# Splitting the first attention's output projection along its contraction, with part of it multiplied between the attention units

## The reference, cut to what matters

```python
def block_fn(args):
    ...
    p = jax.nn.softmax(jnp.concatenate([s_band, s_ctx, s_sink_lat], axis=-1), axis=-1)
    ...
    o = jnp.einsum('bhgqk,bkhd->bqhgd', p_band, vb) + jnp.einsum('bhgqk,bkhd->bqhgd', p_ctx, vc)
    return o

o_blocks = lax.map(block_fn, (jnp.arange(nb), q_blocks))
o_lat = jnp.moveaxis(o_blocks, 0, 1).reshape(bsz, seq, N_HEADS * HEAD_DIM) @ w_o
...
h_lat = h_lat + g1 * y_lat
b_lat = modulate(rmsnorm(h_lat, norm2_g[i]), sh2, sc2)
```

## Time and profile before

| | |
|---|---|
| median of 3 runs | 2436.53 us |
| lowest, highest run | 2434.88, 2446.08 us |
| profiled execution, first to last instruction (its span) | 2433.2 us |
| that execution's own time | not given apart from its span |
| PE (TensorE matmul) busy in the span | 2276.1 us, 94% |
| PEld (weight load), DVE, ACT, POOL busy | 77%, 48%, 41%, 35% |
| first attention, first score to first `wo` matmul | 1042.7 to 1182.5 us |
| stage `wo` | 1182.5 to about 1225 us |

### The profile page before, as it was taken

How to read it: one execution, slowest core, us unless ns; L and a number is a source line. 1 busy time by engine, 2 the same in 40 slices (tenths; PEclk the granted TensorE clock), 3 DMA queues, 4 the chain that set the end, 5 groups by cost and what they waited for, 6 DMA issues and landing times.

```text
span 2433.2 us, 37255 instructions
## 1 busy us (share of the span) xinstructions
PE 2276.1 (94%) x14435; PEld 1872.0 (77%) x14435; DVE 1161.3 (48%) x2028; ACT 987.4 (41%) x1673; POOL 852.0 (35%) x445
## 2 busy tenths in 40 slices
PE   4999699999999998999989999989988889999998
PEld 4887487888888886767778888877746777778777
DVE  4699723432043335378444223447475536441441
ACT  5665544332133324378454324444353214332341
POOL 1799224222222234300144444433301114443443
PEclk9999798999999998999999999999898989999999
DMA  8888021222122221200123333332200002333332
GB/s 272 257 270 255 20 61 52 61 64 72 56 61 60 74 66 58 69 10 1 43 86 97 101 90 95 106 99 79 83 1 2 2 1 86 88 101 90 88 106 83
DMA packets 337090, 204.59 MB, mean 84 GB/s; under 512 B 5869, under 2 KB 335159, under 8 KB 336951
## 3 DMA queue, kind: packets, MB, share of 16 engines
q1 hardware_dynamic: 331915, 194.02, 26.7%
q10 hardware_dynamic: 5036, 8.66, 1.1%
HBM read 200.47 MB, written 2.19 MB: 83 GB/s over the span
## 4 chain that ended last, share of the span: by engine, by line
PE 60%; issue 20%; POOL 9%; DVE 5%; ACT 3%; DVEq 1%; SPq 1%; DMA 1%; ACTq 1%; POOLq 0%
PE ps L623 17%; PE ps L624 17%; PE ps L625 17%; POOL w_lo L550 6%; POOL pc L1610 2%; DVE ps L1578 1%; PE ps L1981 1%; PE ps L896 1%; DVE m L3209 1%; PE ps L2009 1%; PE ps L3008 1%; ACT w_hi L593 1%; DMA ada_x<-in_ada_w 1%; PE ps L1670 1%; SPq L774 0%
## 5 line engine op out<-in xcount | busy, mean ns | idle before, releaser
L550 POOL TENSOR_TENSOR w_lo<-raw,w_hi 128x1024 fp32r<-128x1024 f32 (+1 forms) x203 | 525.8, 2591 | 1105.4 <-ACT w_hi L593 1089.4
L623 PE MATMUL ps<-x_hi,w_hi 128*128 128x512 f32 (+1 forms) x1896 | 689.7, 364 | 30.3 <-DVE x_lo L1481 12.5
L624 PE MATMUL ps<-x_lo,w_hi 128*128 128x512 f32 (+1 forms) x1896 | 676.1, 357 | 0.0
L625 PE MATMUL ps<-x_hi,w_lo 128*128 128x512 f32 (+1 forms) x1896 | 674.6, 356 | 0.0
L593 ACT ACTIVATE w_hi<-raw 128x1024 fp32r<-128x1024 f32 (+1 forms) x251 | 280.3, 1117 | 520.3 <-PE ps L625 515.1
L623 PEld LDWEIGHTS ps<-x_hi,w_hi 128*128 128x128 f32 x1896 | 364.7, 192 | 98.1 <-issue 22.7
L624 PEld LDWEIGHTS ps<-x_lo,w_hi 128*128 128x128 f32 x1896 | 365.4, 193 | 52.3 <-issue 3.8
L625 PEld LDWEIGHTS ps<-x_hi,w_lo 128*128 128x128 f32 x1896 | 364.6, 192 | 50.2
L1855 DVE SCALAR_TENSOR_TENSOR f_a<-ps,prm,f_a 128x511 f32<-128x511 f32 (+2 forms) x176 | 116.1, 680 | 371.4 <-ACT f_b L1820 360.5
L623 PE MATMUL ps<-g_hi,w_hi 128*128 128x512 f32 (+1 forms) x704 | 257.1, 365 | 2.1 <-POOL w_lo L550 1.4
L624 PE MATMUL ps<-g_lo,w_hi 128*128 128x512 f32 (+1 forms) x704 | 255.8, 363 | 0.0
(11 more groups left out here) (388 smaller groups left out, 2966.0 us busy)
## 6 DMA issues: line engine op xcount, KB each, us to landing
raw<-in_ffn_w_up SPq DMA_DIRECT2D x88, 512.0 KB, 3.8
ada_tail<-in_ada_w SPq DMA_DIRECT2D x22, 1024.0 KB, 7.4
raw<-in_ffn_w_down SPq DMA_DIRECT2D x32, 704.0 KB, 4.6
raw<-in_w_up SPq DMA_DIRECT2D x44, 512.0 KB, 3.8
ada_s<-in_ada_w SPq DMA_DIRECT2D x20, 1024.0 KB, 7.9
raw<-in_conv_w_pw SPq DMA_DIRECT2D x24, 512.0 KB, 6.2
raw<-in_w_down SPq DMA_DIRECT2D x16, 704.0 KB, 4.6
raw<-in_w_in SPq DMA_DIRECT2D x17, 512.0 KB, 4.0
```

The costliest lines, as they stand in the source:

```text
L550: pool.tensor_tensor(M.w_lo[:, slot, 0:K * P], M.raw[:, slot, 0:K * P], M.w_hi[:, slot, 0:K * P].bitcast(F32), ALU.subtract).then_inc(lo_r ...
L623: pe.matmul(o, wh, hi[:, k, t0:t0 + tn], start=first, stop=False)
L624: pe.matmul(o, wh, lo[:, k, t0:t0 + tn], start=False, stop=False)
L625: return pe.matmul(o, wl, hi[:, k, t0:t0 + tn], start=False, stop=last)
```

## The change

The projection is now two streams. `woa` has 8 parts: K tiles 0 to 3 of output tiles 0 to 5, and K tiles 4 and 5 of output tiles 0 and 1. `wo` keeps the rest: K tiles 6 and 7 for output tiles 0 and 1, K tiles 4 to 7 for tiles 2 to 5, all eight for tiles 6 and 7 (`PARTS_OF`). The parts of `woa` are multiplied from unit step 40 on, one part in three steps: a third of its matmuls after the products of the first step, a third after the scores of each of the next two. The result gathers in PSUM bank 6, so the transposed pieces of this attention turn over two banks instead of three (`turn_banks=2`). Four steps after a part began, DVE adds it to `h`, and ACT rounds the weights of the part two ahead; POOL's subtraction and SP's load follow by the semaphores as before. Loads, roundings and subtractions are as wide as the part.

```diff
-STREAMS += [("qkv", 12, 8), ("wo", 8, 8)]
+STREAMS += [("qkv", 12, 8), ("woa", 8, 4), ("wo", 8, 8)]
...
+PARTS_OF = {"woa": [(m, 0, 4) for m in range(6)] + [(0, 4, 6), (1, 4, 6)],
+            "wo": [(m, (6, 6, 4, 4, 4, 4, 0, 0)[m], 8) for m in range(8)]}
...
-            sp.dma_start(M.raw[:, slot, 0:K * P].rearrange("p (k c) -> p k c", c=P),
-                         w_src[name][:, :, bass.ds(c, P)]).then_inc(s_raw[slot], 16)
+            k0, k1 = part_of(name, 4 * it + u)[1:] if name in PARTS_OF else (0, K)
+            sp.dma_start(M.raw[:, slot, 0:(k1 - k0) * P].rearrange("p (k c) -> p k c", c=P),
+                         w_src[name][:, k0:k1, bass.ds(c, P)]).then_inc(s_raw[slot], 16)
...
         def turn_ps(self, j):
-            return (TURN_BANK + j % 3) * 512
+            return (TURN_BANK + j % self.turn_banks) * 512
...
         for u in range(n_u + VALUES + 3):
             if u + 2 < n_u:
                 scores(u + 2)
+            if between:
+                between(u, 0)
             if 0 <= u - TURN < n_u:
                 turn(u - TURN)
             for quarter in range(4):
                 for g in X.groups_at(u, VALUES + quarter):
                     values(g, quarter)
+            if between:
+                between(u, 1)
...
-    ATT1 = Attention(groups1(), M.p1, M.pt1, (0, 0, 0, 0, 0))
+    ATT1 = Attention(groups1(), M.p1, M.pt1, (0, 0, 0, 0, 0), turn_banks=2)
+    WOA_BANK, WOA_AT, WOA_UNITS = 6, 40, 3
+    WOA = PARTS_OF["woa"]
...
+        def third(i, n):
+            _, k0, k1 = WOA[i]
+            todo = [(k, x) for k in range(k0, k1) for x in range(3)]
+            if n == 0:
+                pe.wait_ge(lo_ready, done(q0 + i + 1))
+                pe.wait_ge(evac, done(q0 + i))
+                pe.wait_ge(att_x, done(2 * k1))
+            for k, x in todo[n * len(todo) // 3:(n + 1) * len(todo) // 3]:
+                at = slice((k - k0) * P, (k - k0 + 1) * P)
+                w = (M.w_hi, M.w_hi, M.w_lo)[x][:, (q0 + i) % 2, at]
+                mm = pe.matmul(woa_ps(), w, (M.x_hi, M.x_lo, M.x_hi)[x][:, k, 0:SEQ], start=(k, x) == todo[0],
+                               stop=(k, x) == todo[-1])
+            if n == 2:
+                mm.then_inc(tile_done, 1)
+
+        def between(u, late):
+            i, n = (u - WOA_AT) // WOA_UNITS, (u - WOA_AT) % WOA_UNITS
+            if 0 <= i < len(WOA) and late == (n == 0):
+                third(i, n)
...
+        def between(u):
+            i, n = (u - WOA_AT - 4) // WOA_UNITS, (u - WOA_AT - 4) % WOA_UNITS
+            if n or not 0 <= i < len(WOA):
+                return
+            m = WOA[i][0]
+            dve.wait_ge(tile_done, done(q0 + i + 1))
+            o = M.h[:, m, 0:SEQ]
+            dve.scalar_tensor_tensor(out=o, in0=woa_ps(), scalar=M.mods[:, 48 + 16 + m, 0:1], in1=o, op0=ALU.mult,
+                                     op1=ALU.add).then_inc(evac, 1)
...
+            if n == 0 and 0 <= i < len(WOA):
+                high(act, "woa", i // 4, i % 4)
```

More of the change, by code:

```diff
@@ L80, with part_of @@
 N_CHUNKS = dict((s[0], s[1]) for s in STREAMS)
+PARTS_OF = {"woa": [(m, 0, 4) for m in range(6)] + [(0, 4, 6), (1, 4, 6)],
+            "wo": [(m, (6, 6, 4, 4, 4, 4, 0, 0)[m], 8) for m in range(8)]}
+for _name, _parts in PARTS_OF.items():
+    for _i, (_m, _k0, _k1) in enumerate(_parts):
+        ROWS_AT[Q0[_name] + _i] = _k1 - _k0
+def part_of(name, i):
+    return PARTS_OF[name][i] if name in PARTS_OF else (i, 0, ROWS_OF[name])
 Q_ALL = _q
@@ L480, in build_in @@
         order = order[:order.index(stop) + 1]
-    streams_of = {"pw1": ["pw1"], "pw2": ["pw2"], "qkv": ["qkv"], "wo": ["wo"],
+    streams_of = {"pw1": ["pw1"], "pw2": ["pw2"], "qkv": ["qkv"], "attn": ["woa"], "wo": ["wo"],
                   "w_in": ["mem_kv", "w_in"], "w_out": ["w_out"]}
@@ L492, in build_in @@
     w_src = {"pw1": rows(A["conv_w_pw1"][0], 8), "pw2": rows(A["conv_w_pw2"][0], 8),
-             "qkv": rows(A["attn_w_qkv"][0], 8), "wo": rows(A["attn_w_o"][0], 8),
+             "qkv": rows(A["attn_w_qkv"][0], 8), "wo": rows(A["attn_w_o"][0], 8), "woa": rows(A["attn_w_o"][0], 8),
              "w_in": rows(A["w_in_2"][0], 8), "mem_kv": rows(A["w_mem_kv_2"][0], 8),
@@ L508, in column @@
             return W_IN_ORDER[4 * it + u] * P
+        if name in PARTS_OF:
+            return part_of(name, 4 * it + u)[0] * P
         if name.startswith("up"):
@@ L523, in one @@
             sp.wait_ge(lo_ready, done(q0 + 4 * it + u - 1))
-            sp.dma_start(M.raw[:, slot, 0:K * P].rearrange("p (k c) -> p k c", c=P),
-                         w_src[name][:, :, bass.ds(c, P)]).then_inc(s_raw[slot], 16)
-        if full >= 2 and name not in ("qkv", "w_in"):
+            k0, k1 = part_of(name, 4 * it + u)[1:] if name in PARTS_OF else (0, K)
+            sp.dma_start(M.raw[:, slot, 0:(k1 - k0) * P].rearrange("p (k c) -> p k c", c=P),
+                         w_src[name][:, k0:k1, bass.ds(c, P)]).then_inc(s_raw[slot], 16)
+        if full >= 2 and name not in ("qkv", "w_in") and name not in PARTS_OF:
             with sp.Fori(0, full) as it:
@@ L547, in one @@
             slot = (q0 + u) % 2
+            w = ROWS_AT[q0 + 4 * it + u] * P if name in PARTS_OF else K * P
             pool.wait_ge(hi_ready, done(q0 + 4 * it + u + 1))
-            pool.tensor_tensor(M.w_lo[:, slot, 0:K * P], M.raw[:, slot, 0:K * P],
-                               M.w_hi[:, slot, 0:K * P].bitcast(F32), ALU.subtract).then_inc(lo_ready, 1)
+            pool.tensor_tensor(M.w_lo[:, slot, 0:w], M.raw[:, slot, 0:w],
+                               M.w_hi[:, slot, 0:w].bitcast(F32), ALU.subtract).then_inc(lo_ready, 1)
         if last is not None:
@@ L555, in low_stream @@
             return
-        if full >= 2:
+        if full >= 2 and name not in PARTS_OF:
             with pool.Fori(0, full) as it:
@@ L611, in moved, with tile_products @@
         return (M.xg_hi, M.xg_lo) if name.startswith("up2") else (M.x_hi, M.x_lo)
-    def tile_products(pe, name, u, t0, tn, k, at=None, ends=None):
+    def tile_products(pe, name, u, t0, tn, k, at=None, ends=None, k0=0):
         K, q0 = ROWS_OF[name], Q0[name]
@@ L617, in tile_products @@
         hi, lo = moved(name)
-        wh = M.w_hi[:, slot, k * P:(k + 1) * P]
-        wl = M.w_lo[:, slot, k * P:(k + 1) * P]
+        wh = M.w_hi[:, slot, (k - k0) * P:(k - k0 + 1) * P]
+        wl = M.w_lo[:, slot, (k - k0) * P:(k - k0 + 1) * P]
         at = t0 if at is None else at
@@ L637, in products @@
         for n, (t0, tn) in enumerate(segs):
+            if name in PARTS_OF:
+                _, k0, k1 = part_of(name, 4 * it + u)
+                for k in range(k0, k1):
+                    mm = tile_products(pe, name, u, t0, tn, k, ends=(k == k0, k == k1 - 1), k0=k0)
+                continue
             for k in range(ROWS_OF[name]):
@@ L1942, in build_in, with __init__ @@
     class Attention:
-        def __init__(self, groups, p, pt, before):
+        def __init__(self, groups, p, pt, before, turn_banks=3):
             self.groups, self.p, self.pt = groups, p, pt
+            self.turn_banks = turn_banks
             self.units = [x for g in groups for x in g.heads]
@@ L1970, in turn_ps, with att_pe @@
         def turn_ps(self, j):
-            return (TURN_BANK + j % 3) * 512
-    def att_pe(pe, X):
+            return (TURN_BANK + j % self.turn_banks) * 512
+    def att_pe(pe, X, between=None):
         n_u = len(X.units)
@@ L1988, in turn @@
                 j = X.piece[u] + m
-                if j >= 3:
-                    eng, count = X.pieces[j - 3]
+                if j >= X.turn_banks:
+                    eng, count = X.pieces[j - X.turn_banks]
                     if eng == "A":
@@ L2036, in bring_out, with att_dve @@
                  M.ps[:, at:at + nk].rearrange("p (t k) -> p t k", k=P)).then_inc(brought, 1)
-    def att_dve(dve, X):
+    def att_dve(dve, X, between=None):
         n_u = len(X.units)
@@ L2070, in att_dve @@
                 negated(u)
+            if between:
+                between(u)
             if 0 <= u - 1 < n_u:
@@ L2076, in att_dve, with att_act @@
                 low(g)
-    def att_act(act, X):
+    def att_act(act, X, between=None):
         n_u = len(X.units)
@@ L2283, in groups1, with woa_ps, woa_pe, woa_dve @@
         return out_
-    ATT1 = Attention(groups1(), M.p1, M.pt1, (0, 0, 0, 0, 0))
+    ATT1 = Attention(groups1(), M.p1, M.pt1, (0, 0, 0, 0, 0), turn_banks=2)
+    WOA_BANK, WOA_AT, WOA_UNITS = 6, 40, 3
+    WOA = PARTS_OF["woa"]
+    def woa_ps():
+        return M.ps[:, WOA_BANK * 512:(WOA_BANK + 1) * 512]
+    def woa_pe(pe):
+        q0 = Q0["woa"]
+        def third(i, n):
[16 more added lines that the diff above has]
+                third(i, n)
+        return between
+    def woa_dve(dve):
+        q0 = Q0["woa"]
+        def between(u):
[7 more added lines that the diff above has]
+                                     op1=ALU.add).then_inc(evac, 1)
+        return between
+    def woa_act(act):
```

(5 more changed lines are left out.)

8 lines of the change are left out of this document (4 added, 4 removed).

## The result

The changed kernel takes **2441.19 us** (median of 20 runs, 2437.94 to 2450.88) against 2436.46 for the kernel before (20 runs beside it): a ratio of 1.0018, 95% interval 1.0011 to 1.0026. That is 4.7 us more where 1.4 were forecast: no change by the bound of 0.5%, inside the range, and yet the interval excludes the forecast's own size (1.0006). The profiled execution of the changed kernel has a span of 2440.5 us and took 2442.34.

A forecast was written before the change was run, and what follows sets the result against it. TensorE was taken to bound attention and wo. Terms 19.1 - 19.1 + 0.9 + 1.7 - 0.8 - 0.4 = +1.4 us on the median of 2436.5 gave 2437.9 us, range 2430 to 2446.

The forecast's parts named there:

- Moved matmuls: 84 matmuls go from stage wo to the attention, charged in full: -19.1 us in wo, +19.1 in the attention.
- The first rival: In the attention, added matmuls take the place of weight-load pauses: 13.3 us go, 2424.6 us; chance 0.06.
- Waits in wo: In stage wo TensorE waits for weights: +0.9 us before chunk 2, +1.7 before chunk 6, -0.8 at chunk 7.
- End of qkv: Last rounding before the copy of V covers 512 columns, 0.61 us instead of 1.06: -0.4 us.
- What the parts ask of the other engines: In the attention, DVE's additions (0.75 us) and POOL's subtractions (1.30) per part stay hidden behind TensorE: no cost.
- the second rival: In the attention DVE becomes the bound, its scaling late for the transposes: 15.3 us more, 2453.2 us; chance 0.06.
- costs nothing new: After wo the clock's fall to 0.79 of its upper level comes from a pause still there: no added cost.
- The third rival: In the attention, parts wait for DVE to empty bank 6 at 7 handovers: 5.3 us lost, 2443.2; chance 0.04.

The follow-up runs named there:

- few: The changed kernel with 68 of the 84 matmuls moved into the attention left out; 2432.88 us, ratio 0.9969 to the kernel before.
- best: Kernel before, with wo's early K tiles put into TensorE's two pauses and V copied ahead of qkv's last rounding; ratios 0.9991, then 0.9980.

## Why the prediction was right, and where its sum was short

*Moved matmuls.* Forecast +19.1 in the attention; measured 159.01 - 139.82 = +19.2. The first rival, filled pauses, falls with few: 0.1 us of 15.5 at most is left for it. The Trainium skill ("TensorE: Matmul & The Clock Gate", section "Step-by-step: what each phase is for") says that weight loads are pulled ahead of matmuls in flight where the row groups don't conflict or the background buffer is free. The pauses of these passages did not fill up that way.

*Waits in wo.* Forecast +0.9, +1.7, -0.8; measured 0.78, 1.65 and none before chunk 7. The stage's column falls by 16.9, forecast 17.3.

*End of qkv.* Forecast -0.4; the wait went from 1.90 to 1.48. But the column fell by 2.0. The timelines of TensorE, before (over a longer stretch than in the earlier trace rows, so that eight matmuls stand in the row) and changed, each with its stretch's clock:

```profile
1032.31 4.41 PE L2215 MATMUL ps<-k__114,kf 128*128 128x512 f32 x8 [1.90 <-ACT v__113 L2133]
...
1030.50:1036.00 5.50, 3.69 (x7) 2.01 (x8) 0.96 (x1) 2.56 (x3) 2.34 (x1) 0.77 0.09 28
```

```profile
1032.98 2.85 PE L2245 MATMUL ps<-k__114,kf 128*128 128x512 f32 x8 [1.48 <-ACT v__113 L2163]
...
1029.00:1035.00 6.00, 4.52 (x27) 3.54 (x27) 0.00 (x0) 1.75 (x3) 1.26 (x1) 1.00 0.03 9
```

The eight matmuls took 4.41 us in before, at a mean granted clock of 0.77, and 2.85 here, at 1.00. After the longer wait the clock was down in six of seven profiles, after 1.48 or the 0.90 of best in none of seven. That is a gain of 1.6 that I had not put down, and the reason that the touched stages cost +0.3 and not +1.4.

*What the parts ask of the other engines.* In the attention DVE stayed hidden, as forecast: it waited 7.7 us for TensorE's scores from 1127 to 1192. POOL does hold it up, by less than the whole subtraction that I had charged; timelines of POOL and DVE in the changed kernel:

```profile
1137.72 1.28 POOL L566 TENSOR_TENSOR w_lo<-raw,w_hi 128x512 fp32r<-128x512 f32 x1 [104.15 <-ACT w_hi L609]
1146.87 1.28 POOL L566 TENSOR_TENSOR w_lo<-raw,w_hi 128x512 fp32r<-128x512 f32 x1 [7.86 <-ACT w_hi L609]
```

```profile
1138.15 0.87 DVE L2082 TENSOR_TENSOR sm_sum<-sm_sum,sm_e 128x1 f32<-128x1 f32 x1
...
1140.98 0.15 DVE L2082 TENSOR_TENSOR sm_sum<-sm_sum,sm_e 128x1 f32<-128x1 f32 x1
...
1146.97 1.19 DVE L2082 TENSOR_TENSOR sm_sum<-sm_sum,sm_e 128x1 f32<-128x1 f32 x1
```

An addition of one column, 0.15 us otherwise, takes 0.87 and 1.19 beside a subtraction and ends with it, 0.7 and 1.0 us lost where 1.30 were charged. That it lasts over 1 us in steps 44 and after was named as a sign of the second rival; the sign came and the rival did not, since TensorE never waited for DVE's scaling; the waits in few show that the room was not large. The Trainium skill ("SBUF — State Buffer", section "Who interferes with whom") says that a DVE instruction with two SBUF inputs contends with a GpSimd instruction that reads SBUF. The trace agrees, with the 0.87 and 1.19 us.

*What the sum lacked* belongs to the same paragraph of the prediction: DVE's 8 additions were priced by their duration alone, 0.75 us each and hidden. As 8 places in DVE's list they cost 3 to 4 us by the timed runs; the profiles' means put that into the mixers, a stage that I had not looked at. The sentence that the clock "costs nothing new" held behind wo (0.80 in the changed kernel from 1232 to 1258 us, against 0.79), and failed at the end of qkv and in the mixers. Without the moved list the change stands at 1.0002 and 1.0005, +0.5 to +1.2 us, where the sum said +1.4; with it, at +3 to +5. So the mechanism of the touched stages was right. That the total came so near is in part luck: two terms that the sum lacked, -1.6 and +3 to +4, have opposite signs, and the call of no change held because its 0.5% is wider than either.

*The third rival*, late handovers, would have lengthened the attention beyond the added matmuls: +19.2 against 19.1 leaves no room for it.

## What to carry to other kernels

A moved matmul costs the same wherever TensorE sets the pace; what can be gained is a pause, and best fills two of them with the same tiles. When two versions differ by 0.1 to 0.2%, lengthen one engine's list by a few empty instructions before you believe a cause: here 8 drains did as much as the change. And take profiles apart at the same places of the program; the stage that differs need not be one that was edited. But where the clock moves, one profile of a stage proves little: let the timed runs decide.

## What the runs showed of the hardware

I had not expected two things. DVE's list has places about 128 instructions or a multiple of it apart at which the engine pauses, for 0.40 to 0.44 us where no other wait hides it, each with a transfer of an instruction queue behind it; so instructions that cost nothing where they stand can cost something far behind. And with 0.4 us less of a wait, 1.48 instead of 1.90, the granted clock stayed at its upper level for the matmuls that follow, which was worth 1.6 us; behind 1.90 it did so in one profile of seven.
